# GpSimd takes half of the turned products of a state-space loop, and VectorE sums six modulation tiles that TensorE summed

## The chip, the cores and the metric

The kernel runs on one core of a Trainium2 chip. The metric is the device time of one execution in microseconds, from three runs before the change. Everything is float32. The core has TensorE (PE in rows; its weight loads are PEld), VectorE (DVE), ScalarE (ACT), GpSimd (POOL), and the queue engine SyncE (SP), which issues most DMAs.

## The reference, cut to what matters

A sequence of 256 tokens of width 1024 passes two layers. Each layer has a mixer and then a mixture of 16 experts. All of it is modulated by six vectors for each layer, made from a conditioning vector. The second layer's mixer is a complex diagonal state space followed by a gated unit:

```python
cond = jax.nn.silu(c)
for layer in range(DEPTH):
    mod = cond @ ada_w[layer] + ada_b[layer]            # 1024 x 6144
    sh_m, sc_m, g_m, sh_f, sc_f, g_f = jnp.split(mod, 6, axis=-1)
    h = _modulate(_rmsnorm(x, norm_mix_g[layer]), sh_m, sc_m)
    ...
    x = x + g_m[:, None, :] * m
    h = _modulate(_rmsnorm(x, norm_ffn_g[layer]), sh_f, sc_f)
    x = x + g_f[:, None, :] * _hier_moe(h, ...)

def _s5_mixer(h, ...):
    ...
    h_re, h_im = jax.vmap(_s5_scan, in_axes=(None, None, 0, 0))(ab_re, ab_im, bu_re, bu_im)
    y = einsum(h_re, c_re) - einsum(h_im, c_im) + d * u
    act = jax.nn.gelu(y.reshape(B, S, D_MODEL))
    zg = act @ glu_w + glu_b                            # 1024 x 2048
    return zg[..., :D_MODEL] * jax.nn.sigmoid(zg[..., D_MODEL:])
```

## The kernel before

**Modulation.** The two products `cond @ ada_w[layer]` are cut into 24 tiles of 1024x512, 2 MB each. SyncE loads a tile into a ring slot (`send_ada`, L392), and `ada(u, u + 1)` on TensorE (L1638) sums it over its 1024 rows: eight matmuls whose weights are 32 columns that hold `cond` in column `u` and zeros elsewhere. A matmul in float32 is two instructions in the trace. Tiles 0 to 15 are used early. Tiles 16 to 23, of the second layer, stand in the state-space loop. Two of the six vectors that they hold (16, 17: the gate of the mixer) are needed in the gated unit, the others by the experts of layer 2.

**State space.** The stage is a loop over `KD` = 8 blocks of 128 features. For block k, TensorE makes `states(k)` (L2210) in four PSUM banks. VectorE multiplies them by cosine and sine tables (`products(k)`, L1549 to L1552, a PSUM operand and an SBUF one). GpSimd adds and subtracts (L644, L645), except for block 0, where VectorE does. VectorE scans along the sequence (`scans(k)`, L1559, eight scans of 128 elements whose factors and terms are both in SBUF) and turns the result back by the tables (`turned(k)`, L1570 to L1573, four operations on two SBUF tensors each). TensorE then makes `outputs(k)` (L2224, L2225, L2232), and ScalarE applies gelu. Two sets of work tiles (`pr`, `qq`) alternate, so `products(k + 1)` is made before `scans(k)`. Between `states` and `outputs` TensorE has one modulation tile in each turn, and from k = 2 the blocks of the gated unit that are ready.

**Gated unit.** Four pairs (`GLU_PAIRS`) of a value and a gate part, each eight blocks of 128x512 (`glu_blocks`, L2247). ScalarE takes a sigmoid of one part, VectorE multiplies twice and adds to `x` (L1594, L1596, L1294). The experts of layer 2 (`ffn(1)`) begin when `x` is complete.

**Order.** Each engine runs its list in the order in which the code is written; semaphores join them. SyncE issues loads in a written order, each when its slot in a ring of six is free (`free_slot`): the first expert weights of layer 2 go to the slots of tiles 22 and 23 and then to those of the four gated-unit weights.

## Time and profile before

| what | value |
|---|---|
| median of 3 runs | 878.67 us (875.8 to 879.58) |
| the profiled execution, its own time | 876.96 us |
| its span, first to last instruction | 875.2 us |
| mean granted TensorE clock | 0.966 |
| busy: PE, DVE, ACT, POOL | 804.0, 326.0, 189.6, 183.1 us |
| DMA from HBM | 281.64 MB |

The busy time of an engine is a share of the whole. What an edit of one stage is worth is read from that stage: here the stretch from 435 to 555 us, which holds the state-space loop and the gated unit.

### The profile page before, as it was taken

The page shows a single profiled execution, that of the slowest core. Times are in us where ns is not written, and L with a number is a line of the kernel's source. Part 1 is how long each engine was busy: PE and PEld are TensorE (multiplying, and loading weights), DVE is VectorE, ACT ScalarE, POOL GpSimd, SP SyncE. Part 2 cuts the span into 40 slices and gives each one's busy share as a digit, 9 for nine tenths or more (in the row PEclk, how much of TensorE's full clock was granted, in tenths as well). Part 3 has the DMA queues.
Part 4 walks back from the last instruction along what each step waited for, and adds up shares of the span by engine and source line. Part 5 has one row for each costly group of instructions (what it writes and reads, how often), then busy time and mean ns, then how long its engine had stood idle before and what let it go on. Part 6 is the DMA issues. An engine that isn't in the chain of part 4 may idle for free.

```text
span 875.2 us, 12777 instructions
## 1 busy us (share of the span) xinstructions
PE 804.0 (92%) x5191; PEld 449.3 (51%) x5192; DVE 326.0 (37%) x740; ACT 189.6 (22%) x315; POOL 183.1 (21%) x285
## 2 busy tenths in 40 slices
PE   3899979999999999999679999769999999989894
PEld 1367634565465565554555554434444756535441
DVE  1437994461131131311599711342000313214224
ACT  2402330351231221311700110421001203101112
POOL 2518679029400000000123200040011112101000
PEclk9999999999999999999979999869999999999998
DMA  9999999949999999994997792502788799999992
GB/s 322 347 357 387 382 369 342 345 158 422 420 421 422 422 423 422 422 420 204 363 372 264 259 382 97 192 17 100 294 318 304 274 422 417 419 420 420 418 401 76
DMA packets 72263, 289.66 MB, mean 331 GB/s; under 512 B 9302, under 2 KB 10614, under 8 KB 47384
## 3 DMA queue, kind: packets, MB, share of 16 engines
q1 hardware_dynamic: 66784, 279.98, 82.0%
q0 software_dynamic: 4736, 7.35, 2.5%
q10 hardware_dynamic: 696, 1.68, 0.5%
q8 instruction: 33, 0.54, 0.3%
q14 instruction: 14, 0.11, 0.0%
HBM read 281.64 MB, written 13.63 MB: 337 GB/s over the span
## 4 chain that ended last, share of the span: by engine, by line
PE 80%; DMA 9%; DVE 7%; SPq 2%; ACT 1%; issue 1%; DVEq 0%; ACTq 0%
PE PS L1876 20%; PE PS L1897 13%; PE PS L1905 7%; PE PS L2247 7%; PE PS L1879 6%; DMA ring<-in_moe_w 6%; PE PS L1929 4%; PE PS L1834 3%; PE PS L1608 3%; PE PS L1638 3%; DMA ring<-in_ab_w_in 2%; PE PS L1700 2%; PE PS L2232 2%; PE PS L1717 2%; SPq L392 2%; PE PS L2210 1%
## 5 line engine op out<-in xcount | busy, mean ns | idle before, releaser
L1897 PE MATMUL PS<-ring,work 128*64 128x512 f32 (+1 forms) x512 | 129.3, 595 | 2.6 <-DMA ring<-in_moe_w 2.5
L1876 PE MATMUL PS<-ring,hT 128*64 128x256 f32 x896 | 109.2, 386 | 7.4 <-DMA ring<-in_moe_w 7.4
L1876 PE MATMUL PS<-ring,yg 128*64 128x256 f32 x896 | 106.2, 379 | 0.0
L1425 DVE TENSOR_TENSOR work<-work,PS 128x512 f32<-128x512 f32 x32 | 22.0, 688 | 208.2 <-PE PS L1876 158.8
L1876 PEld LDWEIGHTS PS<-ring,hT 128*64 128x64 f32 x896 | 62.7, 138 | 49.1 <-issue 11.8
L1897 PEld LDWEIGHTS PS<-ring,work 128*64 128x64 f32 (+1 forms) x512 | 42.8, 143 | 76.0 <-issue 69.5
L1876 PEld LDWEIGHTS PS<-ring,yg 128*64 128x64 f32 x896 | 64.5, 137 | 32.6 <-issue 0.4
L1905 PE MATMUL PS<-work,xhat 128*128 128x256 f32 (+1 forms) x256 | 66.0, 417 | 4.0 <-issue 4.0
L682 POOL DMA_INDIRECT y_rows<-yg,row_no x24 | 23.4, 974 | 188.4 <-DVE yg L1433 164.9
L1905 PEld LDWEIGHTS PS<-work,xhat 128*128 128x128 f32 x256 | 48.9, 193 | 24.3 <-issue 18.3
L2247 PE MATMUL PS<-ring,yg 128*128 128x512 f32 x128 | 59.4, 615 | 0.0
L913 ACT ACTIVATE work<-PS 128x512 f32<-128x512 f32 x32 | 19.1, 597 | 184.0 <-PE PS L1876 112.9
L1638 PE MATMUL PS<-ring,condz 128*32 128x512 f32 x320 | 40.3, 628 | 11.0 <-DMA ring<-in_ada_w 11.0
L639 POOL DMA_DIRECT2D yg<-in_s_glu_b x4 | 2.5, 634 | 198.2 <-DVE x L1294 198.2
L1462 DVE COPY yg<-PS 128x512 f32<-128x512 f32 x20 | 13.8, 692 | 80.3 <-PE PS L1897 80.3
L2247 PEld LDWEIGHTS PS<-ring,yg 128*128 128x128 f32 x128 | 24.0, 194 | 33.1 <-issue 33.1
L1929 PE MATMUL PS<-yg,grow 64*128 64x512 f32 x160 | 38.4, 608 | 0.0
L1433 DVE SCALAR_TENSOR_TENSOR yg<-PS,rt,work 128x512 f32<-128x512 f32 x24 | 16.9, 747 | 49.4 <-PE PS L1897 49.4
L1834 PE MATMUL PS<-ring,yg 128*128 128x512 f32 x64 | 30.1, 626 | 4.5 <-ACT yg L852 4.5
L927 ACT ACTIVATE yg<-PS 128x512 f32<-128x512 f32 x20 | 12.0, 598 | 85.6 <-PE PS L1897 85.6
L1717 PE MATMUL PS<-hT,ring 128*128 128x256 f32 x128 | 28.9, 382 | 0.0
L1879 PE MATMUL PS<-ring,hT 128*128 128x512 f32 x64 | 28.9, 594 | 0.0
(410 smaller groups left out, 1025.7 us busy)
## 6 DMA issues: line engine op xcount, KB each, us to landing
ring<-in_moe_w SPq DMA_DIRECT2D x96, 2048.0 KB, 16.0
ring<-in_ada_w SPq DMA_DIRECT2D x20, 2048.0 KB, 16.1
work<-in_ada_w SPq DMA_DIRECT2D x4, 2048.0 KB, 14.0
ring<-in_s_glu_w SPq DMA_DIRECT2D x4, 2048.0 KB, 11.8
ring<-in_ab_w_in SPq DMA_DIRECT2D x3, 2048.0 KB, 22.1
ring<-in_ab_w_out SPq DMA_DIRECT2D x2, 2048.0 KB, 15.4
ring<-rot_tables SPq DMA_DIRECT2D x2, 2048.0 KB, 11.2
rot_tables<-grow POOLq DMA_DIRECT2D x8, 256.0 KB, 5.6
```

Of the source, the lines that this page charges most:

```text
L682: g.indirect_dma_start(y_rows[:, :], bass.IndirectOffsetOnAxis(ap=row_no[:, i, e, h:h + 1], axis=0), yg[:, e % 2, h * HALF:(h + 1) * HALF] ...
L1425: v.tensor_tensor(pairs_out(he[:, e % 2, :]), pairs_out(he[:, e % 2, :]), pairs(bank[e % 2 * 2 + 1 if direct else 1]), ALU.mult).then_inc( ...
L1608: return nc.tensor.transpose(dst, src, ident[0:n, 0:n])
L1638: last = mm(bank[7][32 * j:32 * j + 32, :], condz[:, k, 32 - r:64 - r], ada_unit(u)[:, k, :], start=any(first) and k < 4, stop=any(final) ...
L1717: last = mm(dst, w[:, k, :], hT[:, k, :], start=k == 0, stop=k == KD - 1)
L1834: last = mm(bank[2 * b + h], mixT[:, k, b * P:(b + 1) * P], u3(N_WIN + h)[:, k, :], start=k == 0, stop=k == KD - 1)
L1876: last = mm(dst[64 * u:64 * u + 64, 0:256], hg[k][:, e * P:e * P + 64], w[:, k, 256 * u:256 * u + 256], start=k == 0, stop=k == KD - 1)
L1879: last = mm(dst, hg[k][:, e * P:(e + 1) * P], w[:, k, :], start=k == 0, stop=k == KD - 1)
L1897: last = mm(dst, left[:, at:at + (64 if narrow else P)], w[:, c4, h * HALF:(h + 1) * HALF], start=c4 == 0, stop=c4 == KF - 1)
L1905: last = mm(bank[at].rearrange("p (e n) -> p e n", n=P)[:, :, 0:n_s], xhat[:, b, k * P:(k + 1) * P], pick[:, b, :, 0:n_s], start=b == 0, s ...
L1929: last = mm(acc[2 * b + h], pickT[pp, e, b * P:(b + 1) * P], yg[pp, at, h * HALF:(h + 1) * HALF], start=False, stop=False)
L2247: last = mm(bank[GLU_BANK[m][part]], actT[:, k, b * P:(b + 1) * P], u3(n)[:, k, :], start=False, stop=k == KD - 1)
```

## The change

Six of the eight late tiles (18 to 23, `ADA_FOLD` = 18) leave TensorE's loop. VectorE sums each in the gated unit (`fold`): a product and seven multiply-adds of 128x512, each with the one before as input, whose last writes to `folded`. TensorE adds the 128 partitions of the six sums by 24 matmuls with a column of ones (`fold_rows`) in the middle of pair 3. Tiles 16 and 17 are summed between `states(0)`, `states(1)` and the loop. GpSimd takes two of the four turned products and does the sums of block k + 1 ahead of them, instead of just ahead of `scans(k + 1)`. The blocks of the second pair's value part stand in the loop from k = 4, and the gate row too.

```diff
+ADA_FOLD = 18
+SUMMED = lambda k: max(2 * k - 1, 2)
+TURNED = lambda k: min(2 * k + 2, 2 * KD - 1) if k else 1
...
-        GLU_BANK = ((6, 5), (0, 1), (7, 4), (2, 3))
-
-        BATCHES = ((0, ADA_FIRST), (ADA_FIRST, ADA_EARLY), (ADA_EARLY, ADA_ALL))
+        GLU_BANK = ((6, 5), (7, 0), (1, 4), (5, 3))
+        folded = [prods[:, m, :] for m in (0, 2, 4, 1, 3, 5)]
+
+        BATCHES = ((0, ADA_FIRST), (ADA_FIRST, ADA_EARLY), (ADA_EARLY, ADA_FOLD), (ADA_FOLD, ADA_ALL))
...
+                    for j in range(2):
+                        free_slot(ADA_BASE + j)
+                        send_ada(ADA_EARLY + j)
+                    for jj, q in enumerate((0, 2)):
+                        send(GLU_BASE + jj, glu[:, :, q * HALF:(q + 1) * HALF], HALF, HALF)
                     sp_.wait_ge(S("y_ps"), 16)
...
-                    for u in range(ADA_EARLY, ADA_ALL):
+                    for u in range(ADA_FOLD, ADA_FOLD + 2):
                         send_ada(u)
-                        if u == ADA_EARLY + 1:
-                            for jj, q in enumerate((0, 2)):
-                                send(GLU_BASE + jj, glu[:, :, q * HALF:(q + 1) * HALF], HALF, HALF)
                     for jj, q in ((2, 1), (3, 3)):
-                        sp_.wait_ge(S("q_ready"), KD // 2 if jj == 2 else KD)
+                        sp_.wait_ge(S("q_ready"), KD if jj == 2 else 2 * KD)
+                        sp_.wait_ge(S("pool_s5"), TURNED(KD // 2 - 1 if jj == 2 else KD - 1))
                         send(GLU_BASE + jj, glu[:, :, q * HALF:(q + 1) * HALF], HALF, HALF)
+                    for u in range(ADA_FOLD + 2, ADA_ALL):
+                        send_ada(u)
...
-            for k in range(1, KD):
+            def sums(k):
+
                 p_ = pr[k % 2]
                 pool.wait_ge(S("s_used"), k + 1)
-                pool.wait_ge(S("q_ready"), k)
                 g.tensor_tensor(p_[0], p_[0], p_[1], ALU.add)
-                g.tensor_tensor(p_[2], p_[2], p_[3], ALU.subtract).then_inc(S("sum_ready"), 1)
+                g.tensor_tensor(p_[2], p_[2], p_[3], ALU.subtract).then_inc(S("pool_s5"), 1)
+
+            def turned(k):
+
+                m = k % 2
+                pool.wait_ge(S("q_ready"), 2 * k + 1)
+                if k >= 2:
+                    pool.wait_ge(S("y5_ps"), k - 1)
+                g.tensor_tensor(qq[m][:, 0, :], pr[m][1], rot[:, k, 0, :], ALU.mult)
+                g.tensor_tensor(qq[m][:, 3, :], pr[m][3], rot[:, k, 0, :], ALU.mult).then_inc(S("pool_s5"), 1)
+
+            turned(0)
+            sums(1)
+            for k in range(1, KD):
+                if k + 1 < KD:
+                    sums(k + 1)
+                turned(k)
...
                 v.tensor_tensor(f4(p_[0]), bre, f4(c_), ALU.mult)
+                v.tensor_tensor(f4(p_[2]), bim, f4(c_), ALU.mult)
+                if k >= 2:
+                    dve.wait_ge(S("pool_s5"), TURNED(k - 2))
                 v.tensor_tensor(f4(p_[1]), bim, f4(s_), ALU.mult)
-                v.tensor_tensor(f4(p_[2]), bim, f4(c_), ALU.mult)
                 v.tensor_tensor(f4(p_[3]), bre, f4(s_), ALU.mult).then_inc(S("s_used"), 1)
...
-                v.tensor_tensor(qq[m][:, 0, :], gg[0], c_, ALU.mult)
                 v.scalar_tensor_tensor(qq[m][:, 1, :], gg[1], -1.0, s_, ALU.mult, ALU.mult)
-                v.tensor_tensor(qq[m][:, 2, :], gg[0], s_, ALU.mult)
-                v.tensor_tensor(qq[m][:, 3, :], gg[1], c_, ALU.mult).then_inc(S("q_ready"), 1)
-                dve.wait_ge(S("q_ready"), k + 1)
+                v.tensor_tensor(qq[m][:, 2, :], gg[0], s_, ALU.mult).then_inc(S("q_ready"), 1)
+                dve.wait_ge(S("q_ready"), 2 * k + 2)
...
+            def fold(u):
+
+                w, k_of = ada_unit(u), lambda k: condc[:, k:k + 1]
+                dve.wait_ge(S(f"ada_slot_{ADA_SLOT[u]}"), ada_turn(u))
+                link(v.tensor_scalar(w[:, 0, :], w[:, 0, :], k_of(0), None, ALU.mult))
+                for k in range(1, KD - 1):
+                    link(v.scalar_tensor_tensor(w[:, 0, :], w[:, k, :], k_of(k), w[:, 0, :], ALU.mult, ALU.add))
+                if u == ADA_FOLD:
+                    dve.wait_ge(S("pool_s5"), TURNED(KD - 1))
+                v.scalar_tensor_tensor(folded[u - ADA_FOLD], w[:, KD - 1, :], k_of(KD - 1), w[:, 0, :], ALU.mult,
+                                       ALU.add).then_inc(S("ada_used"), 1)
 
             for m, (h, b) in enumerate(GLU_PAIRS):
+                if m < 3:
+                    fold(ADA_FOLD + 2 * m)
+                    fold(ADA_FOLD + 2 * m + 1)
+                else:
+                    mod_evac(3)
+                    mod_scale(3)
                 dve.wait_ge(S("glu_sig"), m + 1)
...
+            def fold_rows():
+
+                pe.wait_ge(S("ada_used"), ADA_ALL)
+                for r in range(ADA_ALL - ADA_FOLD):
+                    for j in range(4):
+                        part = folded[r][:, j::4] if r < 4 else folded[r][:, j * P:(j + 1) * P]
+                        last = mm(bank[2][32 * j:32 * j + 32, 0:P], onez[:, 32 - r:64 - r], part, start=r == 0,
+                                  stop=r == ADA_ALL - ADA_FOLD - 1)
                 last.then_inc(S("ada_cols_ps"), 1)
...
             states(0)
+            ada(ADA_EARLY, ADA_EARLY + 1)
             states(1)
+            ada(ADA_EARLY + 1, ADA_FOLD)
             for k in range(KD):
                 if k + 2 < KD:
                     states(k + 2)
-                ada(ADA_EARLY + k, ADA_EARLY + k + 1)
+                if k == 1:
+                    ada_cols(2)
...
+                if k == 4:
+                    pe.wait_ge(S("mod_cols"), 3)
+                    glu_bias(1, 0, 2)
+                if k >= 4:
+                    glu_blocks(1, 0, 2 * k - 8, min(2 * k - 6, KD - 1))
                 if k == KD - 1:
                     pe.wait_ge(S("s_used"), KD)
-                    glu_bias(1, 0, 0)
                     glu_bias(1, 1, 1)
-                    glu_blocks(1, 0, 0, 3)
+                    gate_row(2)
                 outputs(k)
...
                 for part in range(1 if m == 1 else 0, 2):
-                    glu_blocks(m, part, 0, KD)
+                    if (m, part) == (3, 1):
+                        fold_rows()
+                    glu_blocks(m, part, 0, KD // 2 if (m, part) == (3, 1) else KD)
+                    if (m, part) == (3, 1):
+                        ada_cols(3)
+                        glu_blocks(m, part, KD // 2, KD)
```

The lists of the engines show what stands where. On VectorE, in the turn k = 2 before (`products(3)`, `scans(2)`, `turned(2)`; L1570 to L1573 are the turned products):

```order
L1549 TENSOR_TENSOR work<-PS,ring 128x512 [waits s5_ps,q_ready]
L1550 TENSOR_TENSOR work<-PS,ring 128x512
L1551 TENSOR_TENSOR yg<-PS,ring 128x512
L1552 TENSOR_TENSOR yg<-PS,ring 128x512
L1559 SCALAR_TENSOR_TENSOR work<-s5c,work 128x128 [waits sum_ready]
L1559 SCALAR_TENSOR_TENSOR work<-s5c,work 128x128 x7
L1570 TENSOR_TENSOR work<-work,ring 128x512 [waits y5_ps,dve_order]
L1571 SCALAR_TENSOR_TENSOR work<-work,ring 128x512
L1572 TENSOR_TENSOR work<-work,ring 128x512
L1573 TENSOR_TENSOR work<-work,ring 128x512
```

The same turn of the changed kernel (lines of the changed file: 1592 to 1597 the products, 1604 the scans, 1616 and 1617 what is left of the turned ones):

```order
L1592 TENSOR_TENSOR work<-PS,ring 128x512 [waits s5_ps,q_ready]
L1593 TENSOR_TENSOR yg<-PS,ring 128x512
L1596 TENSOR_TENSOR work<-PS,ring 128x512 [waits pool_s5]
L1597 TENSOR_TENSOR yg<-PS,ring 128x512
L1604 SCALAR_TENSOR_TENSOR work<-s5c,work 128x128 [waits pool_s5]
L1604 SCALAR_TENSOR_TENSOR work<-s5c,work 128x128 x7
L1616 SCALAR_TENSOR_TENSOR work<-work,ring 128x512 [waits y5_ps,q_ready]
L1617 TENSOR_TENSOR work<-work,ring 128x512
```

Two turned products went, and a wait on GpSimd stands in the middle of the products. On GpSimd, over the turns of blocks 1 and 2, the list was two operations a turn:

```order
L644 TENSOR_TENSOR work<-work 128x512 [waits q_ready,s_used]
L645 TENSOR_TENSOR yg<-yg 128x512
L644 TENSOR_TENSOR work<-work 128x512 [waits q_ready,s_used]
L645 TENSOR_TENSOR work<-work 128x512
L644 TENSOR_TENSOR work<-work 128x512 [waits q_ready,s_used]
L645 TENSOR_TENSOR yg<-yg 128x512
```

and is four now (656 and 657 the sums, which wait for the end of the products; 665 and 666 the turned products, which wait for the end of the scans):

```order
L656 TENSOR_TENSOR work<-work 128x512 [waits s_used]
L657 TENSOR_TENSOR work<-work 128x512
L665 TENSOR_TENSOR xhat<-work,ring 128x512 [waits q_ready]
L666 TENSOR_TENSOR xhat<-yg,ring 128x512
L656 TENSOR_TENSOR work<-work 128x512 [waits s_used]
L657 TENSOR_TENSOR yg<-yg 128x512
L665 TENSOR_TENSOR work<-work,ring 128x512 [waits y5_ps,q_ready]
L666 TENSOR_TENSOR work<-work,ring 128x512
```

Behind the loop VectorE's list, once empty up to the first sigmoid, begins with two tiles (1640, 1642, 1645) ahead of the first pair's gating (1656, 1658, 1337); the same nine rows stand three times:

```order
L1640 TENSOR_SCALAR ring<-ring,condc 128x512 [waits ada_slot_0,q_ready]
L1642 SCALAR_TENSOR_TENSOR ring<-ring,condc 128x512 [waits dve_order] x6
L1645 SCALAR_TENSOR_TENSOR work<-ring,condc 128x512 [waits pool_s5,dve_order]
L1640 TENSOR_SCALAR ring<-ring,condc 128x512 [waits ada_slot_1]
L1642 SCALAR_TENSOR_TENSOR ring<-ring,condc 128x512 [waits dve_order] x6
L1645 SCALAR_TENSOR_TENSOR work<-ring,condc 128x512 [waits dve_order]
L1656 TENSOR_TENSOR work<-work,PS 128x512 [waits glu_sig]
L1658 TENSOR_TENSOR work<-work,grow 128x512 [waits grow_ready,dve_order]
L1337 TENSOR_TENSOR x<-x,work 128x512 [waits dve_order]
```

So six tiles in a row, with the gating of two pairs among them, now stand between the last turned product and the matmuls of `fold_rows`.

## Rows read from the trace of the kernel before

**Rows 1.** The chain that ended last, pieces in order: start us, us, what.
```profile
444.09 2.09 PE PS L2210 x32
...
526.27 27.68 PE PS L2247 x64
...
764.13 24.57 DMA ring<-in_moe_w
```
**Rows 2.** Windows: stretch, us; busy of PE, PEld, DVE, ACT, POOL; clock; DMA share, GB/s.
```profile
433.70:446.10 12.40, 5.28 (x96) 4.57 (x96) 10.96 (x22) 3.63 (x9) 0.00 (x0) 0.64 1.05 387
446.10:505.80 59.70, 59.70 (x878) 34.33 (x874) 51.17 (x109) 5.07 (x14) 17.59 (x14) 0.99 0.81 288
505.80:553.90 48.10, 48.10 (x138) 23.14 (x134) 6.67 (x12) 4.56 (x7) 0.00 (x0) 0.96 0.62 242
```
**Rows 3.** Timeline, VectorE, the turn k = 3: start us, us, instructions, idle before.
```profile
462.21 0.69 DVE L1549 TENSOR_TENSOR work<-PS,ring 128x512 f32<-128x512 f32 x1
...
464.86 1.37 DVE L1559 TENSOR_TENSOR_SCAN work<-s5c,work 128x128 f32<-128x128 f32 x4 [0.16 <-POOL yg L645]
...
467.52 0.69 DVE L1570 TENSOR_TENSOR xhat<-work,ring 128x512 f32<-128x512 f32 x1
...
470.06 0.69 DVE L1549 TENSOR_TENSOR work<-PS,ring 128x512 f32<-128x512 f32 x1
```
**Rows 4.** Timeline, GpSimd, in the same turn.
```profile
462.32 1.27 POOL L644 TENSOR_TENSOR work<-work 128x512 f32<-128x512 f32 x1 [5.35 <-DVE work L1573]
463.55 1.27 POOL L645 TENSOR_TENSOR yg<-yg 128x512 f32<-128x512 f32 x1
```
**Rows 5.** Timeline, VectorE: first products of turn k = 1, last turned product.
```profile
446.48 0.69 DVE L1549 TENSOR_TENSOR work<-PS,ring 128x512 f32<-128x512 f32 x1
...
500.83 0.68 DVE L1573 TENSOR_TENSOR xhat<-yg,ring 128x512 f32<-128x512 f32 x1
```
**Rows 6.** Timeline, VectorE, in the first layer, while GpSimd works.
```profile
105.02 0.68 DVE L1272 TENSOR_TENSOR work<-work 128x512 f32<-128x512 f32 x1
...
107.07 2.85 DVE L1272 TENSOR_TENSOR work<-work 128x512 f32<-128x512 f32 x1
109.95 1.64 DVE L1273 TENSOR_TENSOR work<-work 128x512 f32<-128x512 f32 x1
```
**Rows 7.** Timeline, GpSimd, in the same stretch.
```profile
107.28 1.07 POOL L568 TENSOR_TENSOR grow<-work 128x512 f32<-128x512 f32 x1
108.30 1.06 POOL L569 TENSOR_TENSOR work<-work 128x512 f32<-128x512 f32 x1
109.44 1.61 POOL L570 TENSOR_TENSOR grow<-grow,work 128x512 f32<-128x512 f32 x1
```
**Rows 8.** First layer's four scans: timeline, and the line's min/median/max in ns.
```profile
135.59 5.03 DVE L1282 TENSOR_TENSOR_SCAN hT<-work,hT 128x256 f32<-128x256 f32 x4
...
L1282 DVE TENSOR_TENSOR_SCAN hT<-work,hT x4: 660/1448/1699, 135.6 to 140.0; 128x256 f32<-128x256 f32 x4
```
**Rows 9.** Timeline, VectorE and GpSimd, layer 1: an operation between two of GpSimd.
```profile
140.65 1.90 DVE L1285 TENSOR_TENSOR yg<-hT,work 128x1024 f32<-128x1024 f32 x1
...
140.38 1.09 POOL L568 TENSOR_TENSOR grow<-work 128x512 f32<-128x512 f32 x1
141.43 2.03 POOL L569 TENSOR_TENSOR work<-work 128x512 f32<-128x512 f32 x1
```
**Rows 10.** Timeline: an output group and a modulation tile on TensorE; a scaling on VectorE.
```profile
480.29 1.95 PE L2232 MATMUL PS<-work 128*32 128x128 f32 x64
...
483.28 1.92 PE L1638 MATMUL PS<-ring,condz 128*32 128x512 f32 x16
...
427.97 0.75 DVE L1080 TENSOR_SCALAR xhat<-x,stat 128x1024 f32<-128x1024 f32 x1
```
**Rows 11.** DMA issues at 476 to 478 us: KB each, us to landing.
```profile
ring<-in_ada_w SPq DMA_DIRECT2D x1, 2048.0 KB, 8.1
```
**Rows 12.** DMA rate from 400 to 600 us, in slices of 5 us.
```profile
GB/s 367 8 0 187 423 392 385 387 387 360 362 373 367 182 231 231 383 236 393 215 125 410 424 405 316 259 162 3 0 102 324 362 51 0 0 5 3 54 21 0
```

More of the change, by code:

```diff
@@ L295, in build @@
         diagD = w3(o, 2, P); o += 2 * P
+        onez = w3(o, 64); o += 64
         assert o <= T0, o
@@ L309, in build @@
         GLU_PAIRS = ((0, 0), (0, 1), (1, 0), (1, 1))
[L310 to L313 removed]
+        GLU_BANK = ((6, 5), (7, 0), (1, 4), (5, 3))
+        folded = [prods[:, m, :] for m in (0, 2, 4, 1, 3, 5)]
+        BATCHES = ((0, ADA_FIRST), (ADA_FIRST, ADA_EARLY), (ADA_EARLY, ADA_FOLD), (ADA_FOLD, ADA_ALL))
+        arows = (arow0, arow0, arow1, yg[:, 0, 0:P])
         def halves(tab):
@@ L636, in _ @@
             pool.sem_inc(S("h0_ready"), 1)
+            ch.link(g.memset(onez, 0.0))
+            ch.link(g.memset(onez[:, 32:33], 1.0))
             pool.wait_ge(S("x_new"), 2)
@@ L779, in rows_out @@
             def rows_out(i):
-                act.wait_ge(S("ada_used"), BATCHES[i][1])
-                s.activation(arows[i], bank[7], ACT.Copy).then_inc(S("ada_rows"), 1)
+                if i < 3:
+                    act.wait_ge(S("ada_used"), BATCHES[i][1])
+                    s.activation(arows[i], bank[7], ACT.Copy).then_inc(S("ada_rows"), 1)
+                else:
+                    act.wait_ge(S("ada_cols_ps"), 4)
+                    s.activation(arows[i], bank[2][:, 0:P], ACT.Copy).then_inc(S("ada_rows"), 1)
             rows_out(0)
@@ L1010, in _ @@
             for k in range(KD):
+                if k == KD - 1:
+                    gate_row(2)
                 act.wait_ge(S("y5_ps"), k + 1)
@@ L1016, in _ @@
                     diagonal(k + 2)
-                if k == KD - 2:
+                if k == 0:
                     rows_out(2)
             for m, (h, b) in enumerate(GLU_PAIRS):
+                if m == 3:
+                    rows_out(3)
                 act.wait_ge(S("glu_ps"), 2 * m + 2)
                 s.activation(q_a[:, m, :], bank[GLU_BANK[m][1]], ACT.Sigmoid).then_inc(S("glu_sig"), 1)
-                if m == 0:
-                    gate_row(2)
             ffn(1)
@@ L1090, in mod_evac @@
                 lo, hi = BATCHES[i]
-                dve.wait_ge(S("ada_cols_ps"), i + 1)
-                if i:
+                dve.wait_ge(S("ada_cols_ps"), i + 1 if i < 3 else 5)
+                if i == 3:
+                    by_strip = bank[2][:, P:2 * P].rearrange("p (c r) -> p c r", r=32)
+                    m4 = by_c(mod4[:, 1, :, :].rearrange("p s k -> p (s k)"))
+                    v.tensor_tensor(m4, by_strip[:, :, 0:4], m4, ALU.add)
+                    v.tensor_tensor(mod[:, 1, G_F, :].rearrange("p (u c) -> p c u", c=4), by_strip[:, :, 4:6],
+                                    adab[:, 1, G_F * KD:(G_F + 1) * KD].rearrange("p (u c) -> p c u", c=4),
+                                    ALU.add).then_inc(S("mod_cols"), 1)
+                    dve.wait_ge(S("mod_cols"), 4)
+                    return
+                if i == 1:
                     dve.wait_ge(S("cols_ready"), 2)
@@ L1560, in scans @@
                                                     pr[k % 2][2 * w][:, q4 * NJ:(q4 + 1) * NJ], 0.0, ALU.mult, ALU.add)
-                link(last)
+                last.then_inc(S("q_ready"), 1)
+                dve.wait_ge(S("q_ready"), 2 * k + 1)
             def turned(k):
@@ L1644, in ada_cols @@
                 pe.wait_ge(S("ada_rows"), i + 1)
+                if i == 3:
+                    tr(bank[2][:, P:2 * P], arows[3]).then_inc(S("ada_cols_ps"), 1)
+                    return
                 lo, hi = BATCHES[i]
@@ L1649, in ada_cols @@
                               sel[:, r:r + n], start=True, stop=True)
-                if i:
+                if i == 1:
                     f = r + 2
@@ L1654, in ada_cols @@
                                   stop=True)
+                last.then_inc(S("ada_cols_ps"), 1)
+            def fold_rows():
[5 more added lines that the diff above has]
+                                  stop=r == ADA_ALL - ADA_FOLD - 1)
                 last.then_inc(S("ada_cols_ps"), 1)
@@ L1674, in gate_row @@
                 L, sec = n // 2, (G_M if n % 2 == 0 else G_F)
-                pe.wait_ge(S("mod_cols"), (2, 2, 3, 3)[n])
+                pe.wait_ge(S("mod_cols"), (2, 2, 3, 4)[n])
                 at = 4 if n == 0 else 2
@@ L2225, in outputs @@
                 mm(dst[:, 0:NJ], K0[:, k, :], hT[:, k, 0::2], start=False, stop=False)
-                pe.wait_ge(S("q_ready"), k + 1)
+                pe.wait_ge(S("q_ready"), 2 * k + 2)
+                pe.wait_ge(S("pool_s5"), TURNED(k))
                 for w in range(4):
@@ L2282, in _ @@
                     pe.wait_ge(S("grow_ready"), 3)
+                    pe.wait_ge(S("glu_sig"), 1)
                     for q in range(4):
```

12 lines of the change are left out of this document (5 added, 7 removed).

## The prediction

> **What bounds the kernel now.** I read the chain that ended last first. From 444 to 554 us it lies on TensorE: from the third `states` at 444.09 to the last gated-unit matmul, 526.27 + 27.68 = 553.9 [rows 1]. The windows confirm it: TensorE is busy in all of the 59.70 us of the loop and all of the 48.10 us behind it, at nearly the full clock, but in only 5.28 of the 12.40 us ahead of it, while VectorE makes block 0 [rows 2]. VectorE is not far off the bound: 51.17 of 59.70 us. Later the chain passes through loads of expert weights [rows 1], but these loads wait for ring slots that TensorE frees, and in the gated unit the DMA share is 0.62 [rows 2]. No load is late there, so I let a shift of the experts' start pass to the end one to one.
>
> Then I read one turn of VectorE [rows 3]: 7.85 us from 462.21 to 470.06. That is 2.5 of products, a wait of 0.16 for GpSimd, 2.66 of scans (464.86 to 467.52), and 2.54 of turned products. So an operation of 128x512 costs 0.60 in a row (0.69 alone, some 0.72 where each waits for the last). From 446.48 to 501.5 the loop takes 55 us [rows 5]. GpSimd's two sums take 1.27 each, from 462.32 to 464.8, and lie beside the products alone [rows 3, 4]. The products read one operand from PSUM; their spacing beside GpSimd is the usual one and GpSimd's operations aren't longer either.
>
> **The shared price.** The rows of the first layer show what happens where VectorE reads two tensors of SBUF while GpSimd runs. An operation that takes 0.68 at 105.02 takes 2.85 at 107.07, and ends 0.56 behind GpSimd's L569, that is 108.30 + 1.06 = 109.36 [rows 6, 7]. It stood still for both of GpSimd's operations, though it started 0.2 us ahead of the first. The next ones meet too: 1.64 for VectorE, 1.61 for GpSimd against 1.27 for its like. Scans are no exception: four of 0.66 took 5.03 us together, 2.4 more than alone [rows 8]. At 140.65 VectorE came in between two operations of GpSimd, paid 0.7, and GpSimd's second paid 1.0 [rows 9]. So the two take turns by whole operations.
>
> The Trainium skill states this as a rule ("SBUF — State Buffer", section on the two separate sides): VectorE with two SBUF inputs and a GpSimd operation that reads SBUF hold a shared port pair in turn, each for a whole instruction. The rows above agree with it. It speaks against this change, and without it the sum would come to the first rival below.
>
> **The change, part by part.**
>
> *The turn of the loop.* VectorE loses two turned products, 2 x 0.60 = 1.2, and its 0.16 wait, since the sums of the next block are made a turn ahead: 7.85 - 1.36 = 6.5 if nothing met. But the sums now wait for the products' end, and the next thing on VectorE is the scans; GpSimd's turned products wait for the scans' end, and the next thing on VectorE is its own turned products. Both pairs of GpSimd (2 x 1.25 = 2.5) therefore start within some 0.2 us of work that they block, while the products, which they don't block, lie beside an idle GpSimd. For the scans I take 2.3 (2.0 to 2.5: all eight come behind or between the two operations). For the turned pair I take 1.8: 1.2 if VectorE's second operation comes in between, as in [rows 9], 2.5 if it stands for both, as in [rows 6, 7]. The turn is 6.5 + 2.3 + 1.8 = 10.6 us, between 9.7 and 11.5.
>
> *The end of the loop.* Turn k = 1 starts near 446.8 (today 446.48: block 0 has two operations less, and its turned pair meets GpSimd). Six turns of 10.6 are 63.6. The small operations that take modulation columns out of PSUM, now in the loop, are 0.5. The last turn has no products and no sums: 2.66 + 1.2 + 1.8 = 5.7. The loop ends at L = 446.8 + 63.6 + 0.5 + 5.7 = 516.6, against 501.5. In general L = 442.5 + 7p, within half a microsecond, for a turn p.
>
> *TensorE in the loop.* A tile costs 1.9 [rows 10], so eight leave 15.2 us. Tiles 16 and 17 fall into the idle time before 446 [rows 2] and cost nothing; without that cover they would cost 3.8. With at most 7.5 us of work a turn TensorE waits for VectorE in every turn, so what it saves there is worth nothing if p is 10.6.
>
> *The sums on VectorE.* A tile is a scaling (0.75 for 1024 columns [rows 10], so about 0.5 for 512), six operations of 0.72 and one of 0.60: 5.4 us. GpSimd is idle by then. Six are 32.4. Two gatings of 2.1 stand among them, and each second tile waits some 0.8 for a load: a slot is free only when the tile in it is summed, and a load takes 8.1 [rows 11] against 5.4 + 2.1 of other work. The last sum ends at L + 32.4 + 4.2 + 1.5 = L + 38.1 = 554.7.
>
> *TensorE behind the loop.* It has `outputs(7)` 1.95 [rows 10] and, at 0.433 an instruction (27.68 for 64 [rows 1]), 31.3 us of gated unit with its biases before `fold_rows`, so it is there at L + 33.3 = 549.9 and waits some 4.8 us. `fold_rows` is 48 instructions of the shape of the output group's 64 in 1.95: 1.5. Then half a part 3.5, a transpose 0.3, half a part 3.5: L + 38.1 + 8.8 = 563.5. I add 1 us for the clock, which may fall in that wait: the granted clock was 0.64 in the stretch where TensorE had 5.28 of 12.40 us [rows 2]. 564.5 is 10.6 behind today's 553.9.
>
> *At nothing.* The loads of tiles 16 and 17 and of two gated-unit weights move ahead of the tables on SyncE's queue. They fill a hole: the queue moved 8 and 0 GB/s from 405 to 415 [rows 12]. At the 423 GB/s behind it a load of 2 MB is 5 us, so four end near 425, and the first half of the tables, which the first products need at about 435, near 430. If it were late, each microsecond would count in full; I give that no term. Expert weights come later (slot of tile 22 free at about 549), but the experts need them only some 40 us on.
>
> **The sum.** Made against the profiled execution's 876.96 us (the median is 878.67): 876.96 + 10.6 = 887.6; I say **887.5**. In general the time is 876.96 + (L + 47.9) - 553.9 = L + 371, as long as VectorE's chain leads. It breaks even at L = 506, a turn of 9.1. Even with today's turn of 7.85 the six tiles would eat most of the gain.
>
> **Rivals.** A measurement of this kernel can tell about 0.5%, 4.4 us.
>
> *No meeting* (13%): faster. Turns of 6.5 end VectorE's loop at 490, its sums at 528. TensorE then leads. Its 109.8 us from 444.1 lose 15.2 of tiles and about 2 of lowered clock behind today's column matmuls, and gain 1.8 of `fold_rows` and transpose and 1.9 of waits in the first turns: 540.4, 13.5 earlier, 863.5. For it: GpSimd is undisturbed beside the products [rows 4]. Against it: these have a PSUM operand, and [rows 6, 7, 8] are of the kind that counts here.
>
> *They interleave well* (16%): GpSimd's second operation of each pair slips into the products or between scans, so that the turn is 8.5 to 9.6. L is 502 to 510 and the time 873 to 881: from a little faster to no change. For it: [rows 9]. Against it: the sums have no products to lie beside, since they wait for them.
>
> *The forecast* (62%): a turn of 9.7 to 11.5, 881 to 894.
>
> *Worse* (9%): both pairs block in full, and TensorE, with 3 us or more of waits in each turn, works at half the clock, so that its turns or the part behind `fold_rows` cost another 3 to 7 us: 894 to 900.
>
> **Numbers.** Slower by over 0.5%: nearly all of the forecast's case (0.57) and the worse one (0.09), 0.66. Within 0.5%: 0.05 and most of the interleaved case (0.11), 0.16. Faster: 0.18. The range 872 to 896 holds the forecast, the interleaved case and a third of the worse one, 0.81; the forecast's own is 881 to 894.
>
> **What would show it.** In the changed trace: scans that take 4.5 us or more a turn in place of 2.66, with a few of them far above 0.4; one of VectorE's two turned products at 1.8 or 3; a distance of about 10.6 between first products; products still 0.60 apart; the last turned product near 516; TensorE waiting in the loop on VectorE or GpSimd, and at `fold_rows` on the last sum, near 555. Scans at 0.33 spacing throughout would refute the price, and the time would be near 863. A last sum well before TensorE's arrival would refute the second half of the sum.

## The result and the profile after

The changed kernel takes 884.42 us (median of 6 runs, 882.88 to 885.36) against 878.23 of the kernel before on the same chip (6 runs, 875.80 to 879.58): a ratio of 1.0071 (1.0055 to 1.0088), slower by 6.2 us. The profiled execution took 884.29 us with a span of 882.5, against 876.96 and 875.2. VectorE's busy time rose from 326.0 to 372.5 us and GpSimd's from 183.1 to 211.3; TensorE's fell only from 804.0 to 801.8. In the stage itself it fell by 4.8 us (113.1 to 108.3), where six tiles of 1.92 less `fold_rows` would be 9.1; the eight output groups took 19.9 us in place of 15.6, parts of them at a lower clock.

The windows of the changed kernel, with the columns of [rows 2]: busy time of PE, PEld, DVE, ACT and POOL, clock, DMA share and GB/s.

```profile
446.00:511.20 65.20, 53.20 (x721) 37.15 (x714) 64.65 (x97) 4.94 (x14) 42.02 (x28) 0.84 0.18 63
511.20:552.00 40.80, 39.04 (x169) 18.44 (x168) 39.06 (x55) 4.56 (x7) 1.09 (x1) 1.00 0.84 301
```

In [rows 2] TensorE had no idle time in the loop. Here VectorE has next to none (64.65 of 65.20), the loop is longer, TensorE idles for 12 us of it, and its clock is 0.84 there. VectorE stays full for the next 41 us, which is new: before, it was busy for 6.67 of 48.10 us.

One turn of VectorE, the same place as [rows 3], by the timeline (start, duration):

```profile
457.41 0.69 DVE L1592 TENSOR_TENSOR work<-PS,ring 128x512 f32<-128x512 f32 x1
458.02 0.68 DVE L1593 TENSOR_TENSOR yg<-PS,ring 128x512 f32<-128x512 f32 x1
...
459.81 4.68 DVE L1604 TENSOR_TENSOR_SCAN work<-s5c,work 128x128 f32<-128x128 f32 x8
464.53 0.69 DVE L1616 SCALAR_TENSOR_TENSOR work<-work,ring 128x512 f32<-128x512 f32 x1
465.13 1.75 DVE L1617 TENSOR_TENSOR work<-work,ring 128x512 f32<-128x512 f32 x1
...
467.12 0.69 DVE L1592 TENSOR_TENSOR work<-PS,ring 128x512 f32<-128x512 f32 x1
```

And GpSimd beside it, which answers to [rows 4]:

```profile
459.98 1.31 POOL L656 TENSOR_TENSOR work<-work 128x512 f32<-128x512 f32 x1 [1.47 <-DVE yg L1597]
461.25 1.38 POOL L657 TENSOR_TENSOR yg<-yg 128x512 f32<-128x512 f32 x1
464.57 1.77 POOL L665 TENSOR_TENSOR work<-work,ring 128x512 f32<-128x512 f32 x1 [1.94 <-DVE work L1604]
466.31 1.71 POOL L666 TENSOR_TENSOR work<-work,ring 128x512 f32<-128x512 f32 x1
```

The eight scans take 4.7 us in place of 2.66, beside the two sums. Of the two turned products left, the second takes 1.75 in place of 0.69, beside GpSimd's pair, and GpSimd's own turned products take 1.71 to 1.77 where an undisturbed operation is 1.27. The products keep their spacing of 0.6. The turn is 467.12 - 457.41 = 9.7 with the small modulation column in it, and 9.53 without (from 467.12 to 476.65).

The statistics of the two lines (min/median/max in ns, first and last start) say that this holds for the whole loop:

```profile
L1604 DVE TENSOR_TENSOR_SCAN work<-s5c,work x48: 390/398/1441, 440.4 to 507.1; 128x128 f32<-128x128 f32 x48
...
L1617 DVE TENSOR_TENSOR work<-work,ring x4: 1751/1752/1754, 446.1 to 503.4; 128x512 f32<-128x512 f32 x4
L1617 DVE TENSOR_TENSOR xhat<-work,ring x4: 1748/1752/1753, 455.6 to 509.4; 128x512 f32<-128x512 f32 x4
```

The median scan costs what it did: only those that stand beside GpSimd's work are long, and all eight L1617 are. The last one ends the loop, and the sums follow on VectorE:

```profile
509.42 1.75 DVE L1617 TENSOR_TENSOR xhat<-work,ring 128x512 f32<-128x512 f32 x1
511.20 1.38 DVE L1640 TENSOR_SCALAR ring<-ring,condc 128x512 f32<-128x512 f32 x1
...
518.52 4.69 DVE L1642 SCALAR_TENSOR_TENSOR ring<-ring,condc 128x512 f32<-128x512 f32 x6
523.24 0.75 DVE L1645 SCALAR_TENSOR_TENSOR work<-ring,condc 128x512 f32<-128x512 f32 x1
...
551.19 0.75 DVE L1645 SCALAR_TENSOR_TENSOR work<-ring,condc 128x512 f32<-128x512 f32 x1
```

L is 511.2 and the last sum ends at 551.94. TensorE at that place:

```profile
506.43 2.61 PE L2308 MATMUL PS<-work 128*32 128x128 f32 x64 [2.65 <-POOL work L666]
509.54 3.53 PE L2323 MATMUL PS<-ring,yg 128*128 128x512 f32 x6 [0.50 <-ACT yg L1046]
...
516.71 1.95 PE L2308 MATMUL PS<-xhat,work 128*32 128x128 f32 x64
519.18 9.71 PE L2323 MATMUL PS<-ring,yg 128*128 128x512 f32 x22 [0.52 <-ACT yg L1046]
...
529.89 20.87 PE L2323 MATMUL PS<-ring,yg 128*128 128x512 f32 x48
552.00 2.46 PE L1728 MATMUL PS<-work 128*32 128x128 f32 x48 [1.24 <-DVE work L1645]
554.39 3.70 PE L2323 MATMUL PS<-ring,yg 128*128 128x512 f32 x8
...
558.04 3.60 PE L2323 MATMUL PS<-ring,yg 128*128 128x512 f32 x8
```

It waits 1.24 us for the last sum and ends the gated unit at 561.6, 7.7 behind today's 553.9; the span grew by 7.3. Not all of that is the change's. VectorE's first products of the stage stand in the two traces, before and after, at

```profile
435.04 0.69 DVE L1549 TENSOR_TENSOR work<-PS,ring 128x512 f32<-128x512 f32 x1 [1.45 <-PE PS L2210]
```

```profile
436.59 0.69 DVE L1592 TENSOR_TENSOR work<-PS,ring 128x512 f32<-128x512 f32 x1 [1.45 <-PE PS L2285]
```

so this execution came to the stage 1.5 us later than the one of before. The executions of the experiments came to it at 432.6 to 436.6, some earlier, some later, whatever their edit. Counted from the stage's first products the change costs 7.7 - 1.5 = 6.2 us, which is also the difference of the medians: what is lost in the stage is lost at the end. The 1.5 are those of one execution each, and no run isolates them from the loads that the change moves ahead.

### The profile page after: what moved, and what is told of

The parts are those of the page before. It is cut to its first block, busy times and chain, and to the rows that moved or that the text cites. A ratio compares the mean times of both kernels' runs of the same rounds, so it can differ in the third digit from the quotient of the medians.

```text
span 882.5 us, 12732 instructions
## 1 busy us (share of the span) xinstructions
PE 801.8 (91%) x5136; PEld 451.2 (51%) x5137; DVE 372.5 (42%) x773; ACT 189.6 (21%) x316; POOL 211.3 (24%) x303
## 4 chain that ended last, share of the span: by engine, by line
PE 66%; DVE 18%; DMA 10%; issue 2%; SPq 2%; ACT 1%; POOL 0%; DVEq 0%; POOLq 0%; ACTq 0%
PE PS L1951 19%; PE PS L1972 13%; PE PS L1980 7%; PE PS L1954 6%; DMA ring<-in_moe_w 5%; PE PS L2004 4%; PE PS L1909 3%; DVE work L1604 3%; PE PS L1670 3%; DVE ring L1642 3%; DMA ring<-in_ab_w_in 2%; PE PS L1775 2%; SPq L397 2%; PE PS L1792 2%; DMA y_rows<-yg,row_no 2%
## 5 line engine op out<-in xcount | busy, mean ns | idle before, releaser
L1700 PE MATMUL PS<-ring,condz 128*32 128x512 f32 x224 | 29.9, 663 | 10.8 <-DMA ring<-in_ada_w 10.8
L1604 DVE TENSOR_TENSOR_SCAN work<-s5c,work 128x128 f32<-128x128 f32 x48 | 29.3, 676 | 0.1
```

The source lines that it names most:

```text
L1604: last = v.tensor_tensor_scan(pr[k % 2][2 * w + 1][:, q4 * NJ:(q4 + 1) * NJ], r_, pr[k % 2][2 * w][:, q4 * NJ:(q4 + 1) * NJ], 0.0, ALU.mul ...
L1700: last = mm(bank[7][32 * j:32 * j + 32, :], condz[:, k, 32 - r:64 - r], ada_unit(u)[:, k, :], start=any(first) and k < 4, stop=any(final) ...
```

## The experiments

The theories: A, VectorE and GpSimd hold each other up wherever both read all their inputs from SBUF, which lengthens the loop by some 9 us. B, the loop is longer because of the new order alone (the sums a turn ahead, the waits in between), whoever shares what. C, the sums on VectorE and TensorE's wait for them are the loss. Two groups of runs, each on one chip; the kernel before took 878.04 us (25 runs) beside the first four and 877.88 (23 runs) beside the others. The changed kernel was not run again beside them, so a difference to its 884.42 also holds what lies between chips; the kernel before took 878.23, 878.04 and 877.88 in the three groups. An interval behind a ratio is of 95%.

### The old loop with the sums on VectorE

The change with the loop's split as before: VectorE makes all four turned products, GpSimd the sums alone and when it did before.

```diff
+            for k in range(1, KD):
                 p_ = pr[k % 2]
                 pool.wait_ge(S("s_used"), k + 1)
+                pool.wait_ge(S("q_ready"), 2 * k)
...
+                v.tensor_tensor(qq[m][:, 0, :], gg[0], c_, ALU.mult)
                 v.scalar_tensor_tensor(qq[m][:, 1, :], gg[1], -1.0, s_, ALU.mult, ALU.mult)
-                v.tensor_tensor(qq[m][:, 2, :], gg[0], s_, ALU.mult).then_inc(S("q_ready"), 1)
+                v.tensor_tensor(qq[m][:, 2, :], gg[0], s_, ALU.mult)
+                v.tensor_tensor(qq[m][:, 3, :], gg[1], c_, ALU.mult).then_inc(S("q_ready"), 1)
```

> The changed kernel with the old split of the loop: VectorE makes all four turned products, GpSimd's two sums lie beside the products again; the six tiles stay on VectorE behind the loop. Theory (GpSimd and VectorE take turns wherever VectorE reads two SBUF tensors, and that lengthens the turn of the loop): a turn of 7.6 to 7.9 us in place of 9.5, scans 2.66, the loop's end on VectorE near 500 in place of 511, and since the time of the changed kernel is that end plus 373, some 873 us, faster than both. Rival A (the sums of the six tiles on VectorE are what costs): 880 us or more. Rival B (TensorE's thinner loop and its lower clock cost the time): the loop keeps little of the gain, 880 to 884.

Measured: 877.47 us (12 runs, 875.25 to 879.75), ratio 0.9996 (0.9980 to 1.0012). The turn is 7.87 (470.73 to 478.60), as before. The median is 7 us under the change, but not the gain that I expected. Two rows of its timeline say why.

```profile
497.05 1.37 DVE L1585 TENSOR_TENSOR_SCAN work<-s5c,work 128x128 f32<-128x128 f32 x4 [2.76 <-POOL yg L656]
...
543.09 2.89 PE L1709 MATMUL PS<-work 128*32 128x128 f32 x48 [5.74 <-DVE work L1626]
545.91 4.49 PE L2303 MATMUL PS<-ring,yg 128*128 128x512 f32 x8
```

The last scans have no products ahead of them to cover the sums, so they stand 2.76 us, which I had left out. The kernel before has the same wait (2.77); the change, which makes the sums a turn ahead, does not. The loop ends at 502.2 and the last sum at 543.0. TensorE waits 5.74 us for it, at `fold_rows`, and then needs 4.49 us for eight instructions that took 3.70 in the changed kernel. Its gated unit ends at 553.94, as today's does (from a start of the stage that is 0.7 later). So the six tiles off TensorE gain nothing as they are placed: what TensorE saves it spends at `fold_rows`.

### GpSimd's half by itself

The kernel before with only the loop's split changed; all eight tiles stay on TensorE, so there are no sums on VectorE.

```diff
-                v.tensor_tensor(qq[m][:, 0, :], gg[0], c_, ALU.mult)
                 v.scalar_tensor_tensor(qq[m][:, 1, :], gg[1], -1.0, s_, ALU.mult, ALU.mult)
-                v.tensor_tensor(qq[m][:, 2, :], gg[0], s_, ALU.mult)
-                v.tensor_tensor(qq[m][:, 3, :], gg[1], c_, ALU.mult).then_inc(S("q_ready"), 1)
+                v.tensor_tensor(qq[m][:, 2, :], gg[0], s_, ALU.mult).then_inc(S("q_ready"), 1)
```

> The kernel before with one part of the change alone: GpSimd makes half of the turned products and the sums a turn ahead; all eight modulation tiles stay in TensorE's loop. Theory: a turn of 9.5 us, the loop's end near 511 in place of 501.5, and the time 886 to 888 us, as slow as the whole change or slower. Rival A (the tiles on VectorE cost): 878 us, no change. If nothing met, the loop would be TensorE's at 7.45 a turn and the time 875 to 878.

Measured: 889.10 us (6 runs, 887.38 to 893.08), ratio 1.0129 (1.0102 to 1.0156): 11.1 us slower, the slowest of all the kernels here and a little above the 886 to 888 expected. Its turn:

```profile
456.15 0.69 DVE L1568 TENSOR_TENSOR work<-PS,ring 128x512 f32<-128x512 f32 x1
...
458.55 4.70 DVE L1580 TENSOR_TENSOR_SCAN work<-s5c,work 128x128 f32<-128x128 f32 x8
463.28 0.69 DVE L1592 SCALAR_TENSOR_TENSOR work<-work,ring 128x512 f32<-128x512 f32 x1
463.89 1.75 DVE L1593 TENSOR_TENSOR work<-work,ring 128x512 f32<-128x512 f32 x1
465.68 0.69 DVE L1568 TENSOR_TENSOR work<-PS,ring 128x512 f32<-128x512 f32 x1
```

9.53 us, row for row that of the changed kernel. The loop ends at 509.8, 8.3 us later than before, but the gated unit at 566.7, 12.8 later: `outputs(6)` waits 3.27 us for GpSimd's turned products and then takes 3.50 in place of 1.95, and the rest of TensorE's list stands behind it. C is out as the main cause of the loss: there is no sum here and more loss. What the sums add to it is measured by the last two runs.

### The scans' factors in PSUM

This is the run that tells A from B. On VectorE and GpSimd the order and every wait stay, but for one small copy (0.20 us); only the memory of one small operand changes: from block 3 on the scans read their factor column from PSUM bank 7. For that bank to be free the second pair's value part moves behind the loop on TensorE.

```diff
-                        r_ = s5c[:, 0, 4 * k + q4:4 * k + q4 + 1].to_broadcast([P, NJ])
+                        src = s5c[:, 0, :] if k < 3 else bank[7][:, 0:NQT]
+                        r_ = src[:, 4 * k + q4:4 * k + q4 + 1].to_broadcast([P, NJ])
...
+                    link(v.tensor_copy(bank[7][:, 0:NQT], s5c[:, 0, :]))
```

> The changed kernel, but from block 3 on the scans read their factor column from PSUM bank 7 instead of SBUF, so that they read one SBUF tensor and not two; to keep the bank free, the eight blocks of the second pair's value part move behind the loop on TensorE (6 us more there). Theory (the meeting needs two SBUF inputs on VectorE): turns 1 and 2 stay at 9.5 us with scans of 4.7, turns 3 to 6 come to 7.5 with scans of 2.7 although GpSimd's sums still start with them; GpSimd's sums at 1.27 each; the loop's end near 503, the time 878 to 881. Rival (the scans are slowed by anything else that GpSimd does at that time: semaphores, queue, any SBUF traffic): all turns 9.5 and the time near 890.

Measured: 878.32 us (12 runs, 875.60 to 881.57), ratio 1.0008 (0.9989 to 1.0027), 6 under the change. The run holds both cases side by side. With the factors in SBUF the turn from 446.80 to 456.32 is 9.52 long. From block 3 on, on VectorE:

```profile
468.67 1.35 DVE L1605 TENSOR_TENSOR_SCAN work<-PS,work 128x128 f32<-128x128 f32 x4
469.94 1.34 DVE L1605 TENSOR_TENSOR_SCAN yg<-PS,yg 128x128 f32<-128x128 f32 x4
471.31 0.69 DVE L1617 SCALAR_TENSOR_TENSOR xhat<-yg,ring 128x512 f32<-128x512 f32 x1
471.92 1.76 DVE L1618 TENSOR_TENSOR xhat<-work,ring 128x512 f32<-128x512 f32 x1
473.72 0.69 DVE L1592 TENSOR_TENSOR work<-PS,ring 128x512 f32<-128x512 f32 x1
```

and on GpSimd in the same stretch:

```profile
468.83 1.28 POOL L656 TENSOR_TENSOR work<-work 128x512 f32<-128x512 f32 x1 [1.89 <-DVE work L1597]
470.07 1.27 POOL L657 TENSOR_TENSOR work<-work 128x512 f32<-128x512 f32 x1
471.36 1.78 POOL L665 TENSOR_TENSOR xhat<-work,ring 128x512 f32<-128x512 f32 x1
```

The scans take 2.64 us although both sums lie wholly beside them, and the sums are back at 1.27. The turned products, whose inputs I left in SBUF, cost what they did: 1.76 and 1.78. The turn is 7.45 (466.27 to 473.72), under the 7.85 of [rows 3], and the loop ends at 501.1. A is shown for the scans, 2.05 of the 3.15 us that a turn loses, and B is out for them. For the turned pair's 1.1 no run moves an operand; that it is the same meeting is argued from its rows, which are long beside GpSimd in every order and 0.69 in the first experiment, where GpSimd has none of them. The Trainium skill ties the shared pair to VectorE's operations with two SBUF inputs ("SBUF — State Buffer", section on the two separate sides), and a scan with one of its inputs in PSUM behaves as this says.

### The turned products first

GpSimd makes the turned products of block k before the sums of block k + 1, so that the sums no longer stand beside the scans. The price by A is a short wait ahead of the scans.

```diff
-            turned(0)
-            sums(1)
-            for k in range(1, KD):
+            for k in range(KD):
+                turned(k)
                 if k + 1 < KD:
                     sums(k + 1)
-                turned(k)
```

> The changed kernel with GpSimd's two pairs in the other order: turned(k), then sums(k + 1), so that the sums start beside the products of block k + 2 and not with the scans; VectorE's scans of block k + 1 then wait for them. Theory: the scans are undisturbed at 2.66, the turned pair still costs 1.1, and a wait of 1 to 1.5 us stands before the scans: a turn of 8.6 to 9.0, the loop's end near 506, the time 878 to 881. Rival (the length of the turn is the sum of both engines' work wherever it stands): a turn of 9.5 and 884 us.

Measured: 881.83 us (9 runs, 876.67 to 884.42), ratio 1.0049 (1.0030 to 1.0067). The turn is 477.42 - 468.75 = 8.67, within what was expected, and the scans are short but late:

```profile
472.36 2.63 DVE L1602 TENSOR_TENSOR_SCAN work<-s5c,work 128x128 f32<-128x128 f32 x8 [1.12 <-POOL work L657]
475.02 0.69 DVE L1614 SCALAR_TENSOR_TENSOR work<-work,ring 128x512 f32<-128x512 f32 x1
475.63 1.76 DVE L1615 TENSOR_TENSOR work<-work,ring 128x512 f32<-128x512 f32 x1
```

A wait of 1.12 has taken the place of 2.05 of blocked scans. The last scans have no products ahead of them and wait 3.69, and the loop ends at 503.5, which is 505.9 (near 506 was expected) when the stage starts as in the kernel before. The median is a little above the 878 to 881 expected. The profiled execution was the fastest of its nine, and came to the stage at 432.63, 4.0 us before that of the change.

### The old loop, with `fold_rows` behind the gated unit

The first experiment left TensorE waiting 5.74 us in the middle of the last pair. Here the same kernel has `fold_rows` and the transpose behind the last matmul of the gated unit, into bank 7; ScalarE's and VectorE's parts of it move behind theirs as well.

```diff
-                    if (m, part) == (3, 1):
-                        fold_rows()
-                    glu_blocks(m, part, 0, KD // 2 if (m, part) == (3, 1) else KD)
-                    if (m, part) == (3, 1):
-                        ada_cols(3)
-                        glu_blocks(m, part, KD // 2, KD)
+                    glu_blocks(m, part, 0, KD)
+            fold_rows()
+            ada_cols(3)
```

> The first experiment (old split of the loop, six tiles on VectorE) with fold_rows and its transpose moved from the middle of pair 3 to behind the last gated-unit matmul, where TensorE waits some 4.7 us for x; the modulation columns are then taken after the last gating. In the first experiment TensorE stood 5.7 us at fold_rows and its gated unit ended at 553.9, as before the change. Theory (the tiles on VectorE cost nothing but that wait in the middle): the gated unit ends near 544.4, x near 547.5 to 548 in place of 556.7, and the time is 868 to 870 us, faster than both by 1%. Rival (the sums on VectorE are late for the experts wherever TensorE collects them): 874 us or more.

Measured: **870.16 us** (5 runs, 868.84 to 871.77), ratio 0.9910 (0.9890 to 0.9931). It beats both kernels: 7.7 us under the one before, and just above the 868 to 870 expected.

```profile
516.69 27.73 PE L2301 MATMUL PS<-ring,yg 128*128 128x512 f32 x64
544.36 2.48 PE L1707 MATMUL PS<-work 128*32 128x128 f32 x48
...
550.97 1.69 PE L1665 MATMUL PS<-condz,ident 128*128 128x512 f32 x2 [3.41 <-DVE x L1319]
```

The last blocks are one run of 27.73 us, as in [rows 1], but begin 9.6 us earlier. The last sum (542.75 + 0.75) is in time for 544.36. TensorE has to wait there for `x` in any case.

### Two tiles summed in turn

The fifth kernel with the operations of two tiles alternating, to hide the latency from one to the next.

```diff
+                for k in range(KD):
+                    for u, w in zip(us, ws):
...
-                    fold(ADA_FOLD + 2 * m)
-                    fold(ADA_FOLD + 2 * m + 1)
+                    fold2(ADA_FOLD + 2 * m)
```

> The same as e5, and each pair of tiles is summed with its operations interleaved, so that no operation waits for the one just before it. Theory: a tile's pair takes 10 to 10.6 us in place of 11.8, the last sum ends 3 to 5 us earlier, but TensorE's gated unit leads in e5, so the time stays within 1 us of e5's (867 to 870). Rival (VectorE's chain still leads in e5): 3 us faster than e5.

Measured: 886.74 us (5 runs, 886.06 to 889.02), ratio 1.0106 (1.0085 to 1.0128): a clear miss. VectorE:

```profile
502.65 8.04 DVE L1632 SCALAR_TENSOR_TENSOR ring<-ring,condc 128x512 f32<-128x512 f32 x12
...
525.99 0.88 DVE L1629 TENSOR_SCALAR ring<-ring,condc 128x512 f32<-128x512 f32 x2 [11.92 <-DMA ring<-in_ada_w]
...
549.02 0.88 DVE L1629 TENSOR_SCALAR ring<-ring,condc 128x512 f32<-128x512 f32 x2 [10.82 <-DMA ring<-in_ada_w]
```

The idea does what it should to the pair, 10.1 us (501.85 to 512.0) in place of 2 x 5.9. But both ring slots come free only at the pair's end, where one used to come free half a pair earlier and its load ran beside the other's sum. Each later pair now waits some 11 us, and TensorE 15.42 at `fold_rows`.

### Short sums

The changed kernel, with six of the eight terms of the last four tiles left out. It asks whether TensorE's wait for the sums is the bound.

```diff
-                for k in range(1, KD - 1):
+                for k in range(1, KD - 1 if u < ADA_FOLD + 2 else 1):
```

> The changed kernel with work left out: of the last four tiles only the first and the last of the eight terms are summed, so these modulation values are wrong. VectorE's list behind the loop is 19 us shorter. In the changed kernel TensorE waited 1.24 us at fold_rows and worked at a lower clock behind it (2.46 us for 48 matmuls). Theory (both chains hang on the end of the loop and are level at fold_rows): the time falls by 1.2 to 2.5 us only, to 882 to 883. Rival (the prediction's step, that the last sum leads by 4.8 us): 878 to 880.

Measured: 881.23 us (12 runs, 878.69 to 885.76), ratio 1.0041 (1.0024 to 1.0058), 3.2 under the change.

```profile
548.25 2.46 PE L1728 MATMUL PS<-work 128*32 128x128 f32 x48
```

TensorE has no wait, yet more than half of the loss stays (0.41% of 0.71%): the sums hold the end by some 1 to 3 us, and behind them stands TensorE's own list, held by GpSimd's turned products near the end of the loop. The time lies just under the 882 to 883 of the theory and above the 878 to 880 of the rival. What I expected of the clock was wrong: `fold_rows` takes 2.46 us here without a wait as well, and in both kernels the granted clock was 1.00 there. This execution came to the stage at 433.81, 2.8 us before that of the changed kernel, and ended the gated unit 3.8 before it (557.8). So from the stage's start the missing wait is worth 1.0 us; the medians, over the kernel before each, give 2.6 (0.71% less 0.41%), with intervals of 1.5 us to either side.

### The change, with `fold_rows` behind the gated unit

The whole change with the edit of the fifth kernel.

> The whole change with fold_rows moved as in e5; GpSimd keeps its half of the turned products. TensorE reached fold_rows at 550.8 with 7 us of the gated unit left. Theory: the gated unit ends near 558 in place of 561.7 and the time is 879.5 to 881 us, still slower than before, and 10 to 12 us above e5, which is the price of GpSimd's half by itself. Rival (GpSimd's half costs little once the sums are out of the way): within 4 us of e5.

Measured: 880.22 us (12 runs, 875.75 to 882.13), ratio 1.0021 (1.0006 to 1.0037): 4.2 under the change, as expected. With the fifth kernel it gives the price of GpSimd's half where no wait for the sums hides any of it: 880.22 - 870.16 = 10.1 us.

| VectorE's loop | `fold_rows` in pair 3 | `fold_rows` last | eight tiles on TensorE |
|---|---|---|---|
| as before | 877.5 | 870.2 | 878.0 (before) |
| GpSimd's half | 884.4 (the change) | 880.2 | 889.1 |

Down each column stands the price of GpSimd's half: 6.9, 10.1 and 11.1 us. Along the rows stands the place of the collection: last in place of in pair 3 is worth 7.3 us with the old loop and 4.2 with GpSimd's half.

## Why the prediction was right

The median is 3.1 us under the 887.5 predicted and inside both ranges. The main step held, that GpSimd's half lengthens VectorE's turn and that this sets the end. Two steps did not, the size of the turned pair's price and TensorE's path behind the loop, and their errors went against each other. That the time fell inside the forecast's own 881 to 894 is in part luck: with the measured turn of 9.53 the recorded formulas give L = 509.2 and 880.2 us, just outside. The 4.1 us to the profiled 884.3 are 1.5 of a later start of the stage, 0.5 in L, and 2.1 behind L.

- *The shared price.* Right, and for the scans shown as the cause by the run with their factor in PSUM, not only argued from layer 1. *Scans*: 2.3 forecast, 2.05 measured (4.71 - 2.66, from the first scan to the next operation at 479.05; the other full turns have 4.70 to 4.74). *Turned pair*: 1.8 forecast, 1.1 measured. GpSimd's two operations let VectorE's second one in between, as in [rows 9]; it stood for one of them and not for both, and each of GpSimd's paid 0.44 to 0.5 in its turn. The turn is 9.53, not 10.6, just below the 9.7 at which my forecast's case began. By its turn, and by L from the same start of the stage (509.7), the result lay in the rival that they interleave well, which gave 873 to 881.
- *The end of the loop*: L = 511.2 against 516.6, and 509.7 from the same start of the stage as before. Turn 1 began at 447.9, that is 446.4 in the same count, where 446.8 was forecast. The difference is the turn: six of 9.53 are 6.4 us less than six of 10.6. The last turn is 6.0 where I had 5.7: its scans take 3.61, since they meet the end of GpSimd's turned products of block 6, which I had missed, and its turned pair is cheaper as in the others.
- *The sums.* L + 40.7 against L + 38.1. A multiply-add with a column as its scalar is 0.75 to 0.76 alone and 0.787 where each waits for the last; I had 0.72 from plain operations. A tile is 5.91 in place of 5.4, six are 35.5, two gatings 4.3, and the first scaling meets GpSimd's last operation: 1.38 for 0.48, a meeting that I missed (I had GpSimd idle by then). The load waits of 1.5 are next to nothing: a load lands in 7.8 us, and a sum of 5.9 and a gating cover it almost exactly. In the first experiment one wait of 1.06 is left, in the last run one of 0.91.
- *TensorE behind the loop.* This was the term most mis-sized: a wait of 4.8 forecast, 1.24 measured. I had it at `fold_rows` at L + 33.3, and it came at L + 39.6 (550.8). `outputs(7)` began not at L but 5.5 us later (516.71), behind three blocks of the gated unit (six instructions, two blocks of the first pair and one of the second), a bias and the gate row. They stand ahead of it in the list, and TensorE couldn't begin them earlier: they need the gelu of block 6, and `outputs(6)` waited for GpSimd's turned products until 506.4. So this path does not start at L, as I had it, but at GpSimd's operation one block earlier, and the two chains end almost together.
- *`fold_rows`*: 2.46 us against 1.5. The count of 48 was right, the price per instruction was not that of the output group; why is not shown. I added 1 for the clock, but from 511.2 to 552 it was 1.00; it fell in the loop instead, to 0.84.
- *The sum.* T = L + 371 was forecast and L + 373.1 came: 511.2 + 373.1 = 884.3. With L 5.4 under and the rest 2.1 over, the sum is off by 3.3. The break-even turn was not 9.1: by the measured offset L would have to be 503.9 and the turn 8.8, and the runs put it lower still, between 7.87 (the first experiment, level) and 8.67 (the fourth, 3.8 us slower). In that range TensorE waits longer at `fold_rows` and loses clock by it, 6.31 us of wait in the fourth. So a turn of 9.53 is slower, and not "from a little faster to no change" as that rival had it: by the recorded formulas it costs 3.2 us already, and L and the offset behind it add 2.6.
- *At nothing.* The loads that move ahead of the tables cost nothing that shows: the eight kernels here that have them came to the stage at 432.6 to 436.6, the two without at 435.0 and 435.3. TensorE's two early tiles are covered as well.
- *That even with today's turn the six tiles would eat most of the gain.* The first experiment confirms it: no gain that can be told from none. But it holds for the place of `fold_rows` in pair 3 alone; behind the gated unit the same tiles gain 7.7 us.

## What to carry to other kernels

Before giving part of VectorE's work to GpSimd, ask of each operation what VectorE runs beside it and from which memories. Here the turned pair took 1.2 us a turn off VectorE and cost it 1.1, the sums that moved with it beside the scans cost 2.05 more, beside products with a PSUM operand the same sums cost nothing, and moving one small operand to PSUM was enough to free the scans. Work taken off the bounding engine pays only if its result is collected where that engine waits anyway; moving the collection turned a level kernel into one 0.9% faster. When sums out of ring slots are reordered, count when each slot comes free, not only how long the sums take.
